# RMS norms of a two-layer backbone step: squares as each residual k tile is done, channel sum in column form, k outside in the product that follows

## The chip, the cores and the metric

The kernel runs on one core of one Trainium2 chip. The metric is the device time of one execution in microseconds (us), shown as the median of the runs. The core's engines are called PE (TensorE), DVE (VectorE), ACT (ScalarE), POOL (GpSimd) and SP (SyncE, which only issues transfers here). Each runs its own instruction list in order, and they are held together by semaphores.

## What is computed

The reference is one inference step with two layers over 128 context and 512 latent tokens of width 1024. Layer 0 mixes tokens by a gated DeltaNet and channels by a dense SwiGLU; layer 1 mixes by a short gated convolution and channels by a top-2-of-8 expert SwiGLU.

```
def rmsnorm(x, w):
    y = x * lax.rsqrt(jnp.mean(x * x, axis=-1, keepdims=True) + NORM_EPS)
    return y * w
for i in range(DEPTH):
    sh1, sc1, g1, sh2, sc2, g2 = ...
    h = rmsnorm(x, p["norm_w"][i, 0]) * (1 + sc1) + sh1
    x = x + g1 * mixer(h)
    h = rmsnorm(x, p["norm_w"][i, 1]) * (1 + sc2) + sh2
    x = x + g2 * swiglu_or_experts(h)
return rmsnorm(x, p["final_norm"])
```

So there are five norms, called norm 0 to norm 4 here: 0 before the DeltaNet's input product, 1 before the dense SwiGLU, 2 before the convolution's input product, 3 before the router, 4 at the end.

## The kernel before

The residual `xT` lies in SBUF with channels on the partitions: eight k tiles (KT = 8) of 128 channels by T = 640 tokens. Products are made in *units*. A unit multiplies 256 output channels (m = 0, 1, two tiles of 128; at the end of an expert only one) with all k tiles, in two halves of 320 tokens. For accuracy each weight and each activation is split in a high and a low part, and three of the four cross products are made, so that a unit with eight k tiles has 2 x 8 x 3 x 2 = 96 matmuls (`unit`, L517 to L532). `square_units` and `expert` run the units in pairs; units alternate between two weight buffers and two halves of PSUM.

POOL splits the weights of each unit (`split`: high part L421, low part L424, which reads two SBUF tiles); it may begin with the next unit for a buffer when PE has done the unit before in it. SP loads the raw weights. DVE drains the units that add to the residual: `residual` (L1209) for the DeltaNet's output product and the convolution's output product, called through `out_units`, and a loop in `expert` (L1241) for the down projections, which come in five units (`DOWN`) of 2, 2, 2, 1 and 1 tiles with eleven k tiles each. In the expert layer the residual is added in `add_scattered` (L1590), tile by tile.

A norm is spread over three engines by three functions called `norm`:

- ACT squares the k tiles of `xT` into a pair of buffers `sq` (L888), after a single wait that the whole residual is done. After PE's sum it writes the root `ms`, 128x640 (L890).
- DVE adds the squares up in `rstd` (seven adds, L1142, all after the last residual instruction in its list), later takes the reciprocal of the 128x640 tile (L1145), and then makes for each k tile `hp` (x times weight times rstd, L1154) and, after ACT has made the rounded `a_hi` from it (L898), the rest `a_lo` (L1161). It counts `h_lo` per k tile.
- PE multiplies a 128x128 tile of ones with the sum in `rstd` (two matmuls of 320 columns, L584), which leaves the sum over all channels on every partition.

The first unit behind norms 0, 1 and 2 waits for `h_lo` k tile by k tile, but only in its m = 0 half:

```
for m in range(nm):
    for k in range(kts):
        if m == 0 and after is not None:
            pe.wait_ge(sem("h_lo"), KT * after + (k + 1))
```

Between the dense SwiGLU and norm 2 DVE also runs `modulation(1)` (L1186, L1192), which makes the scale tables `mod` and `alpha` of layer 1. In norm 0 the same function for layer 0 stands ahead of the adds.

## Time and profile before

| | |
|---|---|
| median of 3 runs | 3572.23 us (3570.23 to 3577.03) |
| span of the profiled execution | 3566.9 us |
| PE busy in it | 3105.9 us, 87% of the span |
| DVE, ACT, POOL busy | 39%, 24%, 31% |
| mean granted TensorE clock | 0.871 of full speed |

The profile is of one further execution, for which only the span from the first to the last instruction is known. That span is 5.3 us shorter than the median and 3.3 us shorter than the fastest run; what lies around it (start and end of the program) is not in the trace. The busy share of PE says that it is the engine with the most work, not that it never waits.

### The profile page before, as it was taken

The numbers are of one execution on the slowest core, as the hardware profiler recorded it, in microseconds if no ns is written. First come the engines' busy times: TensorE is split into PE (matmuls) and PEld (weight loads), VectorE is DVE, ScalarE is ACT, GpSimd is POOL, SyncE is SP. The second block draws the span as 40 slices with busy tenths as digits, with TensorE's granted clock in tenths as the row PEclk, the third lists the DMA queues.
The fourth block names the chain that finished last, engine by engine and source line by source line (L and its number), as shares of the span: only waits on it lengthen the run. The fifth ranks groups of instructions, "written<-read, shape, count | busy, mean of one in ns | idle before, by whom it ended". The sixth has DMA issues, their size and how long they took to land.

```text
span 3566.9 us, 51011 instructions
## 1 busy us (share of the span) xinstructions
PE 3105.9 (87%) x20306; PEld 2798.3 (78%) x20306; DVE 1386.0 (39%) x1990; ACT 871.5 (24%) x1266; POOL 1120.6 (31%) x365
## 2 busy tenths in 40 slices
PE   7699888888888887799998797678999999999995
PEld 3499777777777776699998787667878888888784
DVE  0400346654665462411111342453443443443344
ACT  0200223222223221210110200223333333433431
POOL 1256022202220241365665363023232332323320
PEclk9799678767876777899999898689999999999996
DMA  9233201110111020122222121034444444544541
GB/s 296 75 126 110 72 25 51 39 53 18 50 38 53 18 70 16 46 85 61 71 81 66 47 71 36 0 95 149 137 129 136 149 124 130 162 123 135 155 136 53
DMA packets 428010, 311.10 MB, mean 87 GB/s; under 512 B 12146, under 2 KB 393067, under 8 KB 427883
## 3 DMA queue, kind: packets, MB, share of 16 engines
q1 hardware_dynamic: 414698, 286.08, 27.0%
q10 hardware_dynamic: 13184, 23.07, 1.9%
q8 instruction: 110, 1.80, 0.2%
q14 instruction: 18, 0.14, 0.0%
HBM read 294.96 MB, written 14.16 MB: 87 GB/s over the span
## 4 chain that ended last, share of the span: by engine, by line
PE 36%; issue 32%; POOL 12%; DVE 4%; ACT 2%; DMA 1%; DVEq 0%; POOLq 0%; SPq 0%; ACTq 0%
PE psum L529 14%; POOL m_lo L380 9%; PE psum L513 7%; PE psum L666 2%; PE psum L683 2%; PE psum L658 2%; POOL w_hi L421 2%; PE psum L577 2%; PE psum L673 2%; PE psum L508 1%; PE psum L689 1%; POOL w_lo L424 1%; DVE xt L1357 1%; PE psum L776 1%; ACT vn L976 1%
## 5 line engine op out<-in xcount | busy, mean ns | idle before, releaser
L380 POOL TENSOR_TENSOR m_lo<-m_raw,m_hi 128x2048 fp32r<-128x2048 f32 (+1 forms) x81 | 356.5, 4401 | 787.0 <-ACT m_hi L1097 787.0
L760 PE MATMUL psum<-he_hi,m_hi 128*128 128x192 f32 x1584 | 452.7, 286 | 35.0 <-POOL m_lo L380 34.8
L760 PE MATMUL psum<-he_lo,m_hi 128*128 128x192 f32 x1584 | 449.5, 284 | 33.7 <-issue 33.7
L421 POOL TENSOR_TENSOR w_hi<-raw,zero 128x2048 fp32r<-128x2048 f32 (+2 forms) x68 | 249.2, 3665 | 681.5 <-PE psum L529 582.1
L529 PE MATMUL psum<-a_hi,w_hi 128*128 128x320 f32 x1728 | 400.6, 313 | 63.9 <-DVE a_lo L1161 32.8
L760 PE MATMUL psum<-he_hi,m_lo 128*128 128x192 f32 x1584 | 450.0, 284 | 0.0
L529 PE MATMUL psum<-a_lo,w_hi 128*128 128x320 f32 x1728 | 396.9, 311 | 0.0
L529 PE MATMUL psum<-a_hi,w_lo 128*128 128x320 f32 x1728 | 396.5, 311 | 0.0
L1097 ACT ACTIVATE m_hi<-m_raw 128x2048 fp32r<-128x2048 f32 (+1 forms) x164 | 290.4, 1771 | 351.0 <-DMA m_raw<-in_moe_w_dram 278.5
L457 POOL TENSOR_TENSOR ml<-lt,level 128x640 f32<-128x640 f32 x80 | 124.8, 1567 | 782.3 <-PE psum L513 782.1
L760 PEld LDWEIGHTS psum<-he_hi,m_hi 128*128 128x128 f32 x1584 | 320.0, 202 | 41.6 <-issue 41.0
L529 PEld LDWEIGHTS psum<-a_hi,w_hi 128*128 128x128 f32 x1728 | 290.9, 190 | 72.8 <-issue 41.1
L760 PEld LDWEIGHTS psum<-he_hi,m_lo 128*128 128x128 f32 x1584 | 320.0, 202 | 34.2 <-issue 34.2
L424 POOL TENSOR_TENSOR w_lo<-raw,w_hi 128x2048 fp32r<-128x2048 f32 (+2 forms) x68 | 329.3, 4843 | 5.3
L760 PEld LDWEIGHTS psum<-he_lo,m_hi 128*128 128x128 f32 x1584 | 319.6, 202 | 0.1
L529 PEld LDWEIGHTS psum<-a_lo,w_hi 128*128 128x128 f32 x1728 | 292.1, 190 | 0.0
L529 PEld LDWEIGHTS psum<-a_hi,w_lo 128*128 128x128 f32 x1728 | 291.9, 190 | 0.0
L380 DVE TENSOR_TENSOR m_lo<-m_raw,m_hi 128x2048 fp32r<-128x2048 f32 (+1 forms) x82 | 179.5, 2189 | 222.9 <-ACT m_hi L1097 222.9
L1608 DVE TENSOR_TENSOR hid_lo<-m_prod,hid_hi 128x192 fp32r<-128x192 f32 x99 | 147.2, 1486 | 42.6 <-ACT hid_hi L1116 42.6
L1605 DVE TENSOR_TENSOR m_prod<-m_sg,psum 128x192 f32<-128x192 f32 x99 | 35.0, 353 | 308.3 <-ACT m_sg L1114 307.0
L577 PE MATMUL psum<-cond,raw 128*128 128x2 f32 x768 | 120.5, 290 | 27.5 <-DMA raw<-in_mod_w_dram 15.7
L577 PEld LDWEIGHTS psum<-cond,raw 128*128 128x128 f32 x768 | 119.5, 247 | 29.7 <-issue 26.4
(289 smaller groups left out, 5240.2 us busy)
## 6 DMA issues: line engine op xcount, KB each, us to landing
m_raw<-in_moe_w_dram SPq DMA_DIRECT2D x274, 512.0 KB, 4.6
raw<-in_mod_w_dram SPq DMA_DIRECT2D x48, 512.0 KB, 3.9
raw<-in_ffn_w_dram SPq DMA_DIRECT2D x44, 512.0 KB, 4.9
mod_raw<-in_mod_w_dram SPq DMA_DIRECT2D x16, 1024.0 KB, 7.2
raw<-in_dn_w_in_dram SPq DMA_DIRECT2D x32, 512.0 KB, 4.4
m_raw<-in_moe_w_dram SPq DMA_DIRECT2D x54, 256.0 KB, 2.7
raw<-in_sc_w_in_dram SPq DMA_DIRECT2D x24, 512.0 KB, 4.4
projected<-stage ACTq DMA_DIRECT2D x16, 640.0 KB, 3.1
```

Source lines behind the costliest of these rows:

```text
L380: eng.tensor_tensor(m_lo[q][:, 0:n], m_raw[j % 2][:, 0:n], m_hi[q][:, 0:n].bitcast(F32), ALU.subtract)\
L421: pool.tensor_tensor(w_hi[s][:, 0:cols], raw[s][:, 0:cols], zero[:, :].broadcast_to([P, cols]), ALU.add)\
L424: pool.tensor_tensor(w_lo[s][:, 0:cols], raw[s][:, 0:cols], w_hi[s][:, 0:cols].bitcast(F32), ALU.subtract).then_inc(sem("split"), 1)
L457: pool.tensor_tensor(ml[:, d, :, :], lt[:, d, :, :], level[:, l, :].unsqueeze(1).broadcast_to([P, TT, P]), ALU.mult)\
L513: mm = pe.matmul(wide(k)[:, t * P:(t + 1) * P], lhs(t), rhs(t), start=True, stop=True)
L529: mm = pe.matmul(psum[:, 4 * s + 2 * m + a, 0:HALF], w[:, k, m, :], v[:, k, a * HALF:(a + 1) * HALF], start=(k == 0 and n == 0), stop=(k = ...
L577: mm = pe.matmul(psum[:, 7, bass.ds(h * (2 * MOD_PER_HEAD) + (MOD_COL + 2 * i), 2)], w[:, k, :], cond[:, k, :], start=(k == 0), stop=(k == ...
L658: pe.matmul(psum[R, 4 * d, 0:P], cv[:, 1, cols], st[:, kind, d, :], start=True, stop=True).then_inc(sem(f"ks{d}"), 1)
L666: pe.matmul(psum[:, 4 * d + 2, 0:CH], st[:, kind, d, :], qe[:, d, cols], start=True, stop=False)
L760: mm = pe.matmul(psum[:, q, g * CAP:(g + 1) * CAP], w[:, c:c + P], v[:, k, :], start=(k == 0 and n == 0), stop=(k == KT - 1 and n == 2))
L1097: act.activation(m_hi[q][:, 0:n], m_raw[j % 2][:, 0:n], ACT.Copy).then_inc(sem("m_high"), 1)
L1608: dve.tensor_tensor(hid_lo[:, j, :], m_prod[:, :], hid_hi[:, j, :].bitcast(F32), ALU.subtract)\
```

## The change

- **Squares early.** ACT's `norm` now waits before each square until that k tile's residual is done (`pair_done`, `down_done`, or `added` in norm 4). DVE's adds are taken out of its `norm` into `add_square`, which is called right behind the residual instructions of each unit (norms 1, 2, 3) or of each tile (norm 4, one tile behind). For norm 0 the adds stay where they were. The loops of DVE around them (`out_units`, and the loop over the two halves of the dense SwiGLU) are written out. In norm 2 the squares lie in `gate_pair` and the sum in `late_total`, since the usual places are still in use; elsewhere the sum is in `sq_total`.
- **Column form.** PE takes the sum of squares as the stationary side against one column of ones, in five matmuls of one column, so that the channel sums of the 640 tokens stand as 128x5. ACT takes the root of 128x5, DVE the reciprocal of 128x5. To get them back along the free axis, DVE multiplies the identity with that column for each of the five token tiles (128x640, into `hp`), PE multiplies ones with it (two matmuls of 320), and DVE copies the 128x640 result from PSUM into `rstd`.
- **k outside.** In units that wait for `h_lo`, the loop over k is outside and the one over m inside.

The diff, cut:

```
-                for m in range(nm):
-                    for k in range(kts):
+                tiles_ = [(m, k) for m in range(nm) for k in range(kts)] if after is None else \
+                    [(m, k) for k in range(kts) for m in range(nm)]
+                for m, k in tiles_:
                         if m == 0 and after is not None:
                             pe.wait_ge(sem("h_lo"), KT * after + (k + 1))
...
             def norm(q):   # tensor
                 pe.wait_ge(sem("sq_added"), (KT - 1) * (q + 1))
+                for t in range(TT):
+                    mm = pe.matmul(psum[:, 0, t:t + 1], square_sum(q)[:, t * P:(t + 1) * P], ones[:, 0:1],
+                                   start=True, stop=True)
+                mm.then_inc(sem("norm_sum"), 1)
+                pe.wait_ge(sem("rstd"), 3 * q + 2)
                 for a in range(2):
-                    mm = pe.matmul(psum[:, a, 0:HALF], ones[:, :], rstd[:, a * HALF:(a + 1) * HALF],
+                    mm = pe.matmul(psum[:, 2 + a, 0:HALF], ones[:, :], hp[:, 0, a * HALF:(a + 1) * HALF],
...
-            def norm(q, ready, count):   # scalar
-                act.wait_ge(sem(ready), count)
+            def norm(q, ready):
                 for k in range(KT):
+                    ready(k)
...
-                act.activation(two(ms[:, :]), halves(0), ACT.Sqrt, scale=1.0 / D, bias=eps[:, :])\
+                act.activation(rcol[:, :], psum[:, 0, 0:TT], ACT.Sqrt, scale=1.0 / D, bias=eps[:, :])\
...
+            def add_square(q, k):   # vector
+                if k == 0:
+                    return
+                dve.wait_ge(sem("squared"), KT * q + k + 1)
+                if k > 1:
+                    dve.wait_ge(sem("sq_added"), (KT - 1) * q + k - 1)
+                dve.tensor_tensor(square_sum(q), squares(q)[:, 0, :] if k == 1 else square_sum(q),
+                                  squares(q)[:, k % 2, :], ALU.add).then_inc(sem("sq_added"), 1)
...
-                dve.reciprocal(rstd[:, :], ms[:, :]).then_inc(sem("rstd"), 1)
+                dve.reciprocal(rcol[:, :], rcol[:, :]).then_inc(sem("rstd"), 1)
+                dve.wait_ge(sem("rstd"), 3 * q + 1)
+                dve.tensor_tensor(tiles(hp[:, 0, :]), ident.unsqueeze(1).broadcast_to([P, TT, P]),
+                                  rcol[:, :].unsqueeze(2).broadcast_to([P, TT, P]), ALU.mult).then_inc(sem("rstd"), 1)
+                dve.wait_ge(sem("norm_sum"), 2 * q + 2)
+                dve.tensor_copy(two(rstd[:, :]), halves(2)).then_inc(sem("rstd"), 1)
...
-            def out_units(u0, gmod):
-                with dve.Fori(0, 2) as i:
-                    for s in range(2):
-                        residual(i * 2 + (u0 + s), s, i * 4 + 2 * s, 2, gmod)
+            def out_units(u0, gmod, q):
+                for n in range(4):
+                    residual(u0 + n, n % 2, 2 * n, 2, gmod)
+                    for k in (2 * n, 2 * n + 1):
+                        add_square(q, k)
...
                     ins.then_inc(sem("added"), 1)
+                    if last and m > 0:
+                        add_square(4, m - 1)
```

The instruction lists show where things went. First DVE around the last unit of the DeltaNet's output product and norm 1 (`xT` is the residual, `sq` the squares, `same` holds the identity). Before:

```order
L1209 SCALAR_TENSOR_TENSOR xT<-psum,mod,xT 128x128
L1209 ISA
L1209 SCALAR_TENSOR_TENSOR xT<-psum,mod,xT 128x192
L1209 ISA
L1209 SCALAR_TENSOR_TENSOR xT<-psum,mod,xT 128x320
L1215 REGISTER_ALU
L1215 COMPARE_AND_BRANCH
L1142 TENSOR_TENSOR rstd<-sq 128x640
L1142 TENSOR_TENSOR rstd<-rstd,sq 128x640 x6
L1145 RECIPROCAL rstd<-ms 128x640
```

After:

```order
L1171 TENSOR_TENSOR sq_total<-sq_total,sq 128x640 x2
L1244 SCALAR_TENSOR_TENSOR xT<-psum,mod,xT 128x128
L1244 SCALAR_TENSOR_TENSOR xT<-psum,mod,xT 128x192
L1244 SCALAR_TENSOR_TENSOR xT<-psum,mod,xT 128x320
L1244 SCALAR_TENSOR_TENSOR xT<-psum,mod,xT 128x128
L1244 SCALAR_TENSOR_TENSOR xT<-psum,mod,xT 128x192
L1244 SCALAR_TENSOR_TENSOR xT<-psum,mod,xT 128x320
L1171 TENSOR_TENSOR sq_total<-sq_total,sq 128x640 x2
L1176 RECIPROCAL rcol<-rcol 128x5
L1178 TENSOR_TENSOR hp<-same,rcol 128x640
L1181 COPY rstd<-psum 128x640
```

Six of the seven adds moved ahead, between the residual instructions of the units; two are behind the last unit. The reciprocal of 640 elements became three instructions.

DVE behind the last down projection, in norm 2, with the change:

```order
L1171 TENSOR_TENSOR late_total<-late_total,gate_pair 128x640
L1222 TENSOR_TENSOR mod<-psum,col 128x96
L1228 SCALAR_TENSOR_TENSOR alpha<-mod,col 128x16 x2
L1176 RECIPROCAL rcol<-rcol 128x5
L1178 TENSOR_TENSOR hp<-same,rcol 128x640
L1181 COPY rstd<-psum 128x640
```

The last add now stands ahead of `modulation(1)`, whose three instructions stand ahead of the reciprocal.

PE at norm 0 and the first product behind it, before:

```order
L584 MATMUL psum<-rstd,ones 128x320 [waits sq_added,mod_evac]
L584 MATMUL psum<-rstd,ones 128x320
L529 MATMUL psum<-a_hi,w_hi 128x320 [waits h_lo,split,rms]
L529 MATMUL psum<-a_hi,w_hi 128x320
L529 MATMUL psum<-a_lo,w_hi 128x320 x2
L529 MATMUL psum<-a_hi,w_lo 128x320 x2
L529 MATMUL psum<-a_hi,w_hi 128x320 [waits h_lo]
```

and after:

```order
L597 MATMUL psum<-ones,sq_total 128x1 [waits sq_added,mod_evac]
L597 MATMUL psum<-ones,sq_total 128x1 x4
L602 MATMUL psum<-hp,ones 128x320 [waits rstd]
L602 MATMUL psum<-hp,ones 128x320
L542 MATMUL psum<-a_hi,w_hi 128x320 [waits h_lo,split,rstd]
L542 MATMUL psum<-a_hi,w_hi 128x320
L542 MATMUL psum<-a_lo,w_hi 128x320 x2
L542 MATMUL psum<-a_hi,w_lo 128x320 x2
L542 MATMUL psum<-a_hi,w_hi 128x320 x2
L542 MATMUL psum<-a_lo,w_hi 128x320 x2
L542 MATMUL psum<-a_hi,w_lo 128x320 x2
L542 MATMUL psum<-a_hi,w_hi 128x320 [waits h_lo]
```

Five one-column matmuls and a wait were added, and per wait for `h_lo` PE now has twelve matmuls to do instead of six.

## Rows read from the trace of the kernel before

**Rows 1.** What PE waited for: line, waited for, total us, times, longest.
```profile
PE psum L584 <- DVE rstd L1142: 73.3, 5, 22.0
```

**Rows 2.** Timeline of DVE at norm 1: start, us, engine, line, instructions, idle before.
```profile
1444.25 2.18 DVE L1209 SCALAR_TENSOR_TENSOR xT<-psum,mod,xT 128x128 f32 x6 [11.90 <-PE psum L529]
1447.85 5.13 DVE L1142 TENSOR_TENSOR rstd<-sq 128x640 f32<-128x640 f32 x1 [1.43 <-ACT sq L888]
1453.78 5.47 DVE L1142 TENSOR_TENSOR rstd<-rstd,sq 128x640 f32<-128x640 f32 x6 [0.80 <-ACT sq L888]
1462.68 4.15 DVE L1145 RECIPROCAL rstd<-ms 128x640 f32<-128x640 f32 x1 [3.42 <-ACT ms L890]
1466.86 1.94 DVE L1154 SCALAR_TENSOR_TENSOR hp<-xT,alpha,rstd 128x128 f32<-128x128 f32 x4
```

**Rows 3.** Timeline of ACT at norm 1.
```profile
1446.46 1.36 ACT L888 ACTIVATE sq<-xT 128x640 f32<-128x640 f32 x2 [67.58 <-DVE xT L1209]
```

**Rows 4.** Timeline of PE at norm 1.
```profile
1459.31 2.50 PE L584 MATMUL psum<-rstd,ones 128*128 128x320 f32 x4 [15.33 <-DVE rstd L1142]
1469.88 0.87 PE L529 MATMUL psum<-a_hi,w_hi 128*128 128x320 f32 x2 [8.06 <-DVE a_lo L1161]
1470.55 0.73 PE L529 MATMUL psum<-a_lo,w_hi 128*128 128x320 f32 x2
1471.08 0.73 PE L529 MATMUL psum<-a_hi,w_lo 128*128 128x320 f32 x2
...
1481.63 0.56 PE L529 MATMUL psum<-a_hi,w_hi 128*128 128x320 f32 x2 [0.83 <-DVE a_lo L1161]
```

**Rows 5.** Timeline of POOL, last two splits ahead of norm 1.
```profile
1429.98 3.60 POOL L421 TENSOR_TENSOR w_hi<-raw,zero 128x2048 fp32r<-128x2048 f32 x1 [5.75 <-PE psum L529]
...
1444.13 3.60 POOL L421 TENSOR_TENSOR w_hi<-raw,zero 128x2048 fp32r<-128x2048 f32 x1 [5.82 <-PE psum L529]
1447.81 4.49 POOL L424 TENSOR_TENSOR w_lo<-raw,w_hi 128x2048 fp32r<-128x2048 f32 x1
```

**Rows 6.** Timeline of POOL: the next split, when norm 1's first unit is done.
```profile
1490.84 3.60 POOL L421 TENSOR_TENSOR w_hi<-raw,zero 128x2048 fp32r<-128x2048 f32 x1 [38.54 <-PE psum L529]
```

**Rows 7.** Stretches behind norms 0 and 1: busy by engine (x), PEclk, DMA, GB/s.
```profile
147.00:151.00 4.00, 3.98 (x13) 3.24 (x13) 3.93 (x9) 2.25 (x4) 0.00 (x0) 0.50 0.00 0
...
1469.90:1476.00 6.10, 6.08 (x19) 4.94 (x20) 5.99 (x14) 3.38 (x6) 0.00 (x0) 0.51 0.00 0
```

**Rows 8.** Timeline of DVE at norm 2.
```profile
1957.89 1.13 DVE L1241 SCALAR_TENSOR_TENSOR xT<-psum,mod,xT 128x128 f32<-128x128 f32 x3 [8.54 <-PE psum L529]
...
1959.42 2.23 DVE L1192 SCALAR_TENSOR_TENSOR alpha<-mod,col 128x16 f32<-128x16 f32 x2
...
1980.73 1.94 DVE L1154 SCALAR_TENSOR_TENSOR hp<-xT,alpha,rstd 128x128 f32<-128x128 f32 x4
```

**Rows 9.** Timeline of POOL at norm 2.
```profile
1957.93 3.60 POOL L421 TENSOR_TENSOR w_hi<-raw,zero 128x2048 fp32r<-128x2048 f32 x1 [1.35 <-PE psum L529]
1961.61 4.50 POOL L424 TENSOR_TENSOR w_lo<-raw,w_hi 128x2048 fp32r<-128x2048 f32 x1
```

**Rows 10.** Timeline of DVE at norm 3.
```profile
2250.87 2.18 DVE L1209 SCALAR_TENSOR_TENSOR xT<-psum,mod,xT 128x128 f32 x6 [11.90 <-PE psum L529]
...
2256.10 5.47 DVE L1142 TENSOR_TENSOR rstd<-rstd,sq 128x640 f32<-128x640 f32 x6 [0.80 <-ACT sq L888]
```

**Rows 11.** Timeline of DVE at norm 4.
```profile
3524.91 1.01 DVE L1590 SCALAR_TENSOR_TENSOR xT<-psum,mod,xT 128x128 f32<-128x128 f32 x2 [1.93 <-PE psum L735]
...
3529.00 5.47 DVE L1142 TENSOR_TENSOR rstd<-rstd,sq 128x640 f32<-128x640 f32 x6 [0.80 <-ACT sq L888]
```

**Rows 12.** Line L812, small matmuls at the low clock: ns min/median/max, first, last start.
```profile
L812 PE MATMUL psum<-tab,tri x4: 414/415/436, 408.4 to 409.0; 128*128 128x40 f32 x4
```

**Rows 13.** Timeline of ACT and DVE in the router: small instructions.
```profile
2311.38 0.24 ACT L1081 ACTIVATE sm<-sm 128x40 f32<-128x40 f32 x1 [26.35 <-DVE sm L1495]
...
2311.87 0.19 DVE L1498 RECIPROCAL sm<-sm 128x5 f32<-128x5 f32 x1
```

More of the change, by code:

```diff
@@ L103, in build @@
         rtb = sb("rtb", [P, E])
+        rcol = sb("rcol", [P, TT])
         wrt_hi = sb("wrt_hi", [P, KT, E], F32R)
@@ L120, in build @@
             yT = sb("yT", [P, KT, T], F32, fin)
+        with ExitStack() as late:
+            sb("late_gap", [P, (2 * KT - 1) * T], F32, late)
+            late_total = sb("late_total", [P, T], F32, late)
         with ExitStack() as dense:
@@ L227, in two, with squares, square_sum @@
             return ap.rearrange("p (a c) -> p a c", a=2)
+        def squares(q):
+            return gate_pair if q == 2 else sq
+        def square_sum(q):
+            return late_total[:, :] if q == 2 else sq_total[:, :]
         SPANS = [(0, TC, 0), (TC, T, 1)]
@@ L881, in _, with pair_done, down_done @@
         def _(act):
-            def norm(q, ready, count):
-                act.wait_ge(sem(ready), count)
+            def norm(q, ready):
                 for k in range(KT):
+                    ready(k)
                     if k >= 2:
                         act.wait_ge(sem("sq_added"), (KT - 1) * q + max(1, k - 2))
-                    act.activation(sq[:, k % 2, :], xT[:, k, :], ACT.Square).then_inc(sem("squared"), 1)
-                act.wait_ge(sem("norm_sum"), q + 1)
-                act.activation(two(ms[:, :]), halves(0), ACT.Sqrt, scale=1.0 / D, bias=eps[:, :])\
+                    act.activation(squares(q)[:, k % 2, :], xT[:, k, :], ACT.Square).then_inc(sem("squared"), 1)
+                act.wait_ge(sem("norm_sum"), 2 * q + 1)
+                act.activation(rcol[:, :], psum[:, 0, 0:TT], ACT.Sqrt, scale=1.0 / D, bias=eps[:, :])\
                     .then_inc(sem("rms"), 1)
+            def pair_done(u0):
+                return lambda k: act.wait_ge(sem("evacuated"), u0 + k // 2 + 1)
+            def down_done(u0):
+                return lambda k: act.wait_ge(sem("evacuated"), u0 + [n for n, m0, nm in DOWN if m0 <= k < m0 + nm][0] + 1)
             def norm_hi(q, n):
@@ L1023, in _ @@
                     mod_rows(i, s, False)
-            norm(0, "x_evac", TT)
+            norm(0, lambda k: act.wait_ge(sem("x_evac"), TT))
             act.wait_ge(sem("alpha"), 2)
@@ L1060, in _ @@
             act.activation(act_hi[:, 0:H, :], oall[:, :, :], ACT.Copy).then_inc(sem("o_hi"), 1)
-            norm(1, "evacuated", U_FFN)
+            norm(1, pair_done(U_DN_OUT))
             norm_hi(1, 1)
@@ L1064, in _ @@
                 expert(e * PER_EXPERT + U_FFN)
-            norm(2, "evacuated", U_SC_IN)
+            act.wait_ge(sem("multiplied"), U_FFN + PER_EXPERT + FT)
+            norm(2, down_done(U_FFN + PER_EXPERT + FT))
             act.wait_ge(sem("alpha"), 4)
@@ L1076, in _ @@
             act.activation(a_hi[:, :, :], cy[:, :, :], ACT.Copy).then_inc(sem("cy_hi"), 1)
-            norm(3, "evacuated", U_MOE)
+            norm(3, pair_done(U_SC_OUT))
             norm_hi(3, 1)
@@ L1131, in _ @@
                 routed(x)
[L1132 removed]
+            norm(4, lambda k: act.wait_ge(sem("added"), n_items * KT + (k + 3)))
         @block.vector
         def _(dve):
[L1137 to L1146 removed]
+            def add_square(q, k):
[6 more added lines that the diff above has]
+                                  squares(q)[:, k % 2, :], ALU.add).then_inc(sem("sq_added"), 1)
+            def norm(q, w_of, out=None):
+                dve.wait_ge(sem("rms"), q + 1)
+                dve.reciprocal(rcol[:, :], rcol[:, :]).then_inc(sem("rstd"), 1)
[4 more added lines that the diff above has]
+                dve.tensor_copy(two(rstd[:, :]), halves(2)).then_inc(sem("rstd"), 1)
+                dve.wait_ge(sem("rstd"), 3 * q + 3)
                 n = q % 2
@@ L1227, in gate_unit, with expert @@
                                   ALU.subtract).then_inc(sem("act_lo"), 1)
-            def expert(u0, n0):
+            def expert(u0, n0, last):
                 with dve.Fori(0, 5) as i:
@@ L1244, in expert @@
                     ins.then_inc(sem("evacuated"), 1)
+                    for k in range(m0, m0 + nm) if last else ():
+                        add_square(2, k)
             def conv(dst, src, w, tag, n0):
@@ L1398, in _ @@
             modulation(0)
+            for k in range(KT):
+                add_square(0, k)
             norm(0, a_of(0))
@@ L1449, in _ @@
                 .then_inc(sem("act_lo"), 1)
-            out_units(U_DN_OUT, 16)
+            out_units(U_DN_OUT, 16, 1)
             norm(1, a_of(1))
-            with dve.Fori(0, N_FFN) as e:
-                expert(e * PER_EXPERT + U_FFN, e * FT)
+            for e in range(N_FFN):
+                expert(e * PER_EXPERT + U_FFN, e * FT, e == N_FFN - 1)
             modulation(1)
@@ L1583, in gathered_low, with add_scattered @@
                                       ALU.subtract).then_inc(sem("he_lo"), 1)
-            def add_scattered(x):
+            def add_scattered(x, last=False):
                 for m in range(KT):
@@ L1629, in _ @@
                 routed(x)
-            add_scattered(n_items)
-            dve.memset(small[:, 0, 0:1], 0.0).then_inc(sem("moe_done"), 1)
+            add_scattered(n_items, True)
+            add_square(4, KT - 1)
             norm(4, lambda k, w: col1[:, C_FINAL + k:C_FINAL + k + 1], out=yT)
```

27 lines of the change are left out of this document (9 added, 18 removed).

## The prediction

> **What bounds the kernel now.** I read the waits of PE first, then the timeline of each engine around each norm. PE has most of the work, so what can be won without taking work from it is time in which it stands still. The waits name it: the ones-matmul of the norms waited 73.3 us in five places for DVE's adds [rows 1], and PE's first unit behind a norm stands still again, 8.06 us ahead of it and a little ahead of each tile [rows 4]. The timelines show that nothing else runs beside these waits: at norm 1 the last unit ends at about 1444.1, when POOL and DVE are released [rows 2, 5], and PE's next product starts at 1469.88 [rows 4]. So at each norm the end is set by this chain: last residual, squares, adds, sum, root, reciprocal, `hp`, `a_hi`, `a_lo`, first unit. A microsecond taken from it is a microsecond of the kernel, as all later work is released by other work, and in the stage behind it PE has the longest turn: units follow each other every 14.15 us while POOL's two splits need 8.2 [rows 5].
>
> **Squares early.** Call the end of the last add T, measured against the end of the last residual instruction.
>
> Norm 1. Before: residual ends 1446.43, T = 1453.78 + 5.47 = 1459.25 [rows 2]. With the change only adds 6 and 7 are left there. The first add took 5.13 us where the same instruction later takes 0.9 [rows 2]; it began at 1447.85, right behind the start of POOL's second split at 1447.81, and ended 0.7 after that one's end at 1452.30 [rows 5]. So an add with both inputs in SBUF waits for a running POOL instruction to end, then takes 0.7. Square 6 is there at 1447.2 [rows 3], in the first split; add 6 runs from 1447.73 to 1448.4. If the second split slips by that, it ends at 1452.9 and T is 1453.6; if not, 1453.0. The Trainium skill (SBUF — State Buffer, "SBUF: two separate sides") says that of a DVE instruction with two SBUF inputs and a GpSimd one that reads SBUF, whichever starts first holds a shared port pair for its whole length and the other blocks; by that the split does slip. I take 1453.6: **5.6 us** saved (6.2 if it does not slip).
>
> Norm 3. The same list, but POOL has no unit left to split. Residual ends 2253.05, T was 2261.57 [rows 10]. Now: two squares, 1.4, and one add behind them, 0.9, so T = 2255.4: **6.1 us**.
>
> Norm 2. Residual ends 1959.02; DVE then ran `modulation(1)` to 1961.65, and `hp` began at 1980.73 [rows 8]. Now add 7 (its square ready at 1959.8) waits for POOL's first split to end at 1961.53 [rows 9] and ends at 1962.2. The three modulation instructions come behind it, beside PE's five matmuls and ACT's root; but `alpha` has two SBUF inputs too (2.23 us for two 128x16 tiles, until a POOL instruction ended [rows 8, 9]), so it waits for the second split, 1962.3 to 1966.8. The reciprocal comes at about 1967.2, and from there the chain below needs 4.6: `hp` at 1971.8, **9.0 us** earlier.
>
> Norm 4. Residual ends 3525.92, T was 3534.47 [rows 11]. Now add 6 (0.8, its square long done) and add 7 end at 3527.6: **6.9 us**.
>
> Norm 0. The adds stay behind `modulation(0)`, in the same order: 0.
>
> **Cover of the moved adds.** Six adds and squares now lie inside the units. DVE's residual part of a unit takes 2.2 us of a turn of 14.15 [rows 2, 5]; two adds that each sit out a POOL instruction add at most 3.6 + 4.5 + 1.4 = 9.5. That is 11.7, still hidden. If the cover were gone, each microsecond above 14.15 would stop PE in every such unit. ACT is idle there (67.58 us before the first square [rows 3]). In norm 4 a tile comes every 2.9 us, 1.93 idle and 1.01 residual [rows 11]; an add of 0.9 fits.
>
> **Column form.** Before, T to `hp` took 1466.86 - 1459.25 = 7.6 us [rows 2], of which 2.5 PE [rows 4] and 4.15 the reciprocal. Now: five fp32 matmuls of one column. No row shows one; the nearest are L812's, 128x128 weights and 40 columns at the low clock: four records for two instructions, started 0.2 apart, the last 0.41 long [rows 12]. Ten records give 9 x 0.2 + 0.4, with their start 2.3. Root 0.24, reciprocal 0.19 [rows 13] (a 128x40 and the same size). Identity times column 0.9, as an add [rows 2]; PE 0.1 + 2.5 [rows 4]; the copy, 640 elements, again 0.9; handovers 0.1. Sum 7.3: **0.3 us** saved per norm at norms 0, 1, 3, 4 (in norm 2 it is in the 9.0). The chain swaps one long DVE instruction for a second trip through PE and gains nearly nothing. Bounds: if the records run twice as fast, 1 us less; if they cost twice as much, 2.1 us more.
>
> The Trainium skill (FP8 and Floating Point Precision, "TensorE Precision Notes") says that true fp32 takes four passes through the array. The trace has two records for an fp32 instruction, four for two matmuls [rows 4]. Four times the five matmuls would be twenty records, the upper bound just given, and the sum over five norms would be 10 us worse. I go by the rows.
>
> **k outside** (norms 0, 1, 2; norm 3 is followed by the router, which waits for everything, norm 4 by transposes). In norm 1 the first unit ran from 1469.88 to about 1490.8 [rows 4, 6], 20.9 us. Its seventh k tile began at 1481.63 [rows 4], so DVE and ACT deliver `a_lo` every 11.75 / 6 = 1.96 us; behind the last tile come 48 more matmuls, m = 1, at the high clock. PE needs for its twelve matmuls 3.2 us at 1.2 GHz (two start 0.53 apart [rows 4]) or 1.76 at 2.4 GHz (a unit of 96 in 14.15 [rows 5], 0.147 each). So at the low clock PE becomes the slower one, at the high clock it keeps up. The granted clock was 0.51 in the first 6.1 us of that unit, and 0.50 in the first 4 of the one behind norm 0 [rows 7]; the latter I take for norm 2 too. Norm 1: 6.0 us cold hold 22.5 matmuls, the other 73.5 take 10.8, together 16.8: **4.1 us** saved. Norms 0 and 2: 4 us hold 15, the other 81 take 11.9, together 15.9: **5.0 us** each. The floor is `a_lo` of the last tile and twelve matmuls, 1.0 + 1.8 behind that seventh tile (the last needs no `hp` of a next one, half a step), 14.5 in all, so at most 6.4 each. The units behind are released by PE and by POOL, which starts its next split when this unit ends and has 6 us to spare, so all of it moves forward.
>
> **Sum.** 0: 5.3. 1: 5.6 + 0.3 + 4.1 = 10.0. 2: 9.0 + 5.0 = 14.0. 3: 6.4. 4: 7.2. Together **42.9 us**. The span would go from 3566.9 to 3524.0; the median lies 5.3 above the span, and I keep that distance: 3572.2 - 42.9 = **3529.3 us**. What one measurement can tell from no change is about 0.2%, 7 us.
>
> **Rivals.**
>
> A. *The column matmuls cost double.* Twenty passes instead of ten, 2.1 us in each of five norms: 3529.3 + 10.5 = 3540. For: no row has a moving side of one column. Against: L812's records. 8%.
>
> B. *k outside brings nothing,* because PE at the low clock with twelve matmuls per tile stays behind, or the clock rises later than before: 14.1 us lost, 3543. Against: PE was busy for nearly all of those first microseconds already (6.08 of 6.10 [rows 7]), so there is little to rise sooner or later for. 5%.
>
> C. *The change does not bring the squares forward:* ACT's per-tile waits or the buffer waits hold them until the last unit. Then 27.6 + 0.3 of the gain is gone and about 15 stay: 3557. Against: the waits name earlier counts, and ACT is idle. 3%.
>
> D. *Slower than before: the adds inside the units hold DVE longer than PE's turn.* Each add sits out POOL's instructions, the next residual comes late, and PE waits for its PSUM. DVE's turn would be 2.2 + two adds; it decides above 14.15, that is from 6 us per add on. To eat the gain of 43 in the thirteen units with adds (4, 5 and 4 in norms 1, 2, 3) it needs 3.3 us beyond, 7.6 per add; at 8.5 per add it is 5.0 us each, 65 in all, 3529 + 65 = 3594. For: an add took 5.13 against one POOL instruction [rows 2]. Against: that instruction was the longer of the two, and the turns behind a down unit are longer still. 3%.
>
> **How the numbers follow.** My forecast has 81%. Its own bounds: T of norm 1 0.6 better, k outside 1 better, the column 1 better in five places and other handovers, 8 in all: 3521; the other way 1 us in each of ten places: 3539. The range takes in A and B and some spread of the runs (3570 to 3577 before): **3519 to 3545**. It leaves out C, D and a rest. Faster by over 0.2%: 0.94, which is the forecast with A, B, C and less a rest for what I have not seen; within 0.2%: 0.03; slower: 0.03.
>
> **What would show it.** In the profile of the changed kernel: T some 7.2 us behind the last residual at norm 1, 2.4 at norm 3, 1.7 at norm 4; one add of about 5 us beside POOL's second split at norms 1 and 2; T to `hp` at 7.3; five matmuls in 2.3; the first unit behind norms 0, 1 and 2 at 16 to 17 us instead of 20.9; PE's units in the product ahead of norm 1 still 14.15 apart. Wrong would be: T to `hp` above 8.5, adds that end after the next unit, a first unit above 18, or a stage away from the norms that grows.

## The result, and the profile after

The changed kernel takes **3476.5 us** (median of 4 runs, 3472.3 to 3479.2) against 3572.9 of the kernel before in the same job (4 runs, 3570.2 to 3577.0): a ratio of 0.973, 95% interval 0.971 to 0.975. The profiled execution has a span of 3475.1 us instead of 3566.9, 91.8 less. (The two differences are not the same because the profiled execution of the kernel before was a short one; see the heads below.) I had predicted 3529.3 and a range of 3519 to 3545: the sign was right, but the gain is 96 us instead of 43, and the time lies below the range.

Both programs do the same work in the same order, so a start in one trace can be set against the same start in the other. The table cuts the span into six at such marks (ends of named PE work), in us:

| stretch | before | after | difference | predicted |
|---|---|---|---|---|
| to the end of norm 0's first unit | 167.6 | 163.0 | -4.6 | -5.3 |
| to the end of the second DeltaNet head | 490.4 | 502.6 | **+12.2** | 0 |
| heads 3 to 8 | 709.1 | 709.2 | 0.1 | 0 |
| norms 1, 2, 3, with what lies between, to the first expert tile | 1001.1 | 968.6 | -32.5 | -30.4 |
| loop over the routed experts, first to last L760 tile | 1090.7 | 1031.0 | **-59.7** | 0 |
| behind it: last down projection, norm 4, output | 107.9 | 100.7 | -7.2 | -7.2 |

The stretches with norms give 44.3 us where 42.9 were predicted. Two stretches in which the change alters nothing moved too: that is the miss. (The heads are the eight heads of the DeltaNet.)

First what was predicted. What PE waited for, in the changed kernel (line, waited for, total us, times, longest), answers to [rows 1]:

```profile
PE psum L597 <- DVE sq_total L1171: 39.1, 4, 22.0
...
PE psum L602 <- DVE hp L1178: 9.0, 5, 3.2
...
PE psum L597 <- DVE late_total L1171: 4.5, 1, 4.5
```

The waits for the adds fell from 73.3 to 39.1 + 4.5; 22.0 of it is norm 0, where nothing was moved. DVE at norm 1 (start, us, instructions, idle before), against [rows 2]:

```profile
1440.49 6.53 DVE L1171 TENSOR_TENSOR sq_total<-sq_total,sq 128x640 f32<-128x640 f32 x2 [0.81 <-ACT sq L906]
1451.58 2.17 DVE L1244 SCALAR_TENSOR_TENSOR xT<-psum,mod,xT 128x128 f32<-128x128 f32 x6 [4.57 <-PE psum L542]
1454.56 6.45 DVE L1171 TENSOR_TENSOR sq_total<-sq_total,sq 128x640 f32<-128x640 f32 x2 [0.80 <-ACT sq L906]
1463.69 0.19 DVE L1176 RECIPROCAL rcol<-rcol 128x5 f32<-128x5 f32 x1 [2.68 <-ACT rcol L908]
1463.91 0.82 DVE L1178 TENSOR_TENSOR hp<-same,rcol 128x640 f32<-128x640 f32 x1
1467.33 0.82 DVE L1181 COPY rstd<-psum 128x640 f32<-128x640 f32 x1 [2.59 <-PE psum L602]
1468.19 1.94 DVE L1190 SCALAR_TENSOR_TENSOR hp<-xT,alpha,rstd 128x128 f32<-128x128 f32 x4
```

The residual ends at 1453.75 and the last add at 1461.01: T is 7.26 behind it (predicted 7.2), and `hp` begins 7.18 after T (predicted 7.3). (Of the seven adds five lie inside the units, and two behind the last; that six moved, as the text ahead of the prediction and the prediction have it, is a miscount. It enters no term.) The adds inside the units end long before the next residual: 1440.49 + 6.53 = 1447.02 against 1451.58, still 14.08 behind the one before. POOL at the same norm, against [rows 5, 6]:

```profile
1451.69 3.60 POOL L433 TENSOR_TENSOR w_hi<-raw,zero 128x2048 fp32r<-128x2048 f32 x1 [5.36 <-PE psum L542]
1455.37 4.96 POOL L436 TENSOR_TENSOR w_lo<-raw,w_hi 128x2048 fp32r<-128x2048 f32 x1
1488.01 3.60 POOL L433 TENSOR_TENSOR w_hi<-raw,zero 128x2048 fp32r<-128x2048 f32 x1 [27.68 <-PE psum L542]
```

The two adds end 0.68 behind POOL's second split (1455.37 + 4.96 = 1460.33): one of them sat it out. PE behind norm 1, against [rows 4]:

```profile
1461.06 2.29 PE L597 MATMUL psum<-ones,sq_total 128*128 128x1 f32 x10 [9.52 <-DVE sq_total L1171]
1464.79 2.50 PE L602 MATMUL psum<-hp,ones 128*128 128x320 f32 x4 [1.44 <-DVE hp L1178]
1471.20 0.87 PE L542 MATMUL psum<-a_hi,w_hi 128*128 128x320 f32 x2 [3.91 <-DVE a_lo L1197]
```

Ten records in 2.29 us (predicted 2.3). The first unit runs from 1471.20 to about 1488.0, 16.8 us instead of 20.9. DVE at norms 2 and 4, against [rows 8, 11]:

```profile
1957.10 2.32 DVE L1171 TENSOR_TENSOR late_total<-late_total,gate_pair 128x640 f32<-128x640 f32 x1 [0.80 <-ACT gate_pair L906]
...
1959.62 4.28 DVE L1228 SCALAR_TENSOR_TENSOR alpha<-mod,col 128x16 f32<-128x16 f32 x2
1963.93 0.19 DVE L1176 RECIPROCAL rcol<-rcol 128x5 f32<-128x5 f32 x1
...
1968.43 1.94 DVE L1190 SCALAR_TENSOR_TENSOR hp<-xT,alpha,rstd 128x128 f32<-128x128 f32 x4
```

```profile
3440.33 1.01 DVE L1630 SCALAR_TENSOR_TENSOR xT<-psum,mod,xT 128x128 f32<-128x128 f32 x2 [1.20 <-PE psum L753]
3441.25 1.75 DVE L1171 TENSOR_TENSOR sq_total<-sq_total,sq 128x640 f32<-128x640 f32 x2
```

`alpha` sits out a POOL split again (4.28 us), as foreseen. The add at norm 2 took 2.32: it waited for the first split alone, and is not the add of about 5 us that my list of signs had there.

Now what was not. Part 3 of the page (queue, kind: packets, MB, share) for the kernel before, then for the changed one:

```profile
q8 instruction: 110, 1.80, 0.2%
```

```profile
q8 instruction: 38, 0.62, 0.1%
```

q8 brings PE's code: its packets have 16,384 bytes each, and in straight code the trace has 254 to 256 PE instructions between two of them (in the kernel before at 1648.8, 1667.3, 1686.0 and 1704.5). Before, 69 of the 110 packets fall between 2492 and 3485, in the loop over the experts, nine in a round. Between 2452 and 3430 the changed kernel has one q8 packet. PE's waits in that loop, before:

```profile
PE psum L760 <- issue: 33.7, 8, 4.5
PE psum L760 <- POOL m_lo L380: 27.8, 18, 2.8
PE psum L719 <- POOL m_lo L380: 6.2, 4, 1.7
```

and after:

```profile
PE psum L737 <- POOL m_lo L392: 14.8, 9, 2.5
PE psum L778 <- POOL m_lo L392: 9.4, 9, 1.2
PE psum L778 <- DVE m_lo L392: 1.3, 4, 0.4
```

Eight waits for "issue", one at each jump back of nine rounds, are gone, 33.7 us; the other waits fell by 8.5. One of the eight in PE's timeline, before (eighth matmul of the round):

```profile
2610.70 0.27 PE L760 MATMUL psum<-he_hi,m_hi 128*128 128x192 f32 x1
2615.34 0.25 PE L760 MATMUL psum<-he_lo,m_hi 128*128 128x192 f32 x1 [4.37 <-issue]
2615.43 0.28 PE L760 MATMUL psum<-he_hi,m_lo 128*128 128x192 f32 x1
```

And the loop as a stretch (us, busy by engine, PEclk, DMA share, GB/s), before and after:

```profile
2368.29:3458.98 1090.69, 1022.78 (x7248) 911.46 (x7247) 461.16 (x513) 396.91 (x452) 342.79 (x78) 0.97 0.47 137
```

```profile
2343.37:3374.36 1030.99, 1005.39 (x7249) 894.92 (x7247) 477.11 (x513) 396.29 (x453) 343.56 (x78) 0.99 0.50 143
```

PE is busy 17.4 us less at the same number of matmuls: the granted clock is 0.97 against 0.99. So 33.7 + 8.5 + 17.4 = 59.6 of the 59.7. This is a sum of what differs; which of its terms hang on one cause is for the experiments.

### The profile page after: what moved, and what is told of

It reads as the page before. It is cut to its first block, busy times and chain, and to the rows that moved or that the text cites. A ratio compares the mean times of both kernels' runs of the same rounds, so it can differ in the third digit from the quotient of the medians.

```text
span 3475.1 us, 51066 instructions
## 1 busy us (share of the span) xinstructions
PE 3105.1 (89%) x20356; PEld 2801.9 (81%) x20356; DVE 1412.7 (41%) x1999; ACT 868.6 (25%) x1266; POOL 1125.0 (32%) x365
## 4 chain that ended last, share of the span: by engine, by line
PE 36%; issue 31%; POOL 12%; DVE 4%; ACT 2%; DMA 1%; DVEq 0%; POOLq 0%; SPq 0%; ACTq 0%
PE psum L542 15%; POOL m_lo L392 9%; PE psum L525 7%; PE psum L684 2%; PE psum L701 2%; PE psum L676 2%; POOL w_hi L433 2%; PE psum L691 2%; PE psum L590 2%; PE psum L707 1%; POOL w_lo L436 1%; DVE xt L1395 1%; PE psum L794 1%; ACT vn L1002 1%; PE psum L520 1%
## 5 line engine op out<-in xcount | busy, mean ns | idle before, releaser
L778 PE MATMUL psum<-he_hi,m_hi 128*128 128x192 f32 x1584 | 444.1, 280 | 17.9 <-POOL m_lo L392 16.4
L778 PE MATMUL psum<-he_lo,m_hi 128*128 128x192 f32 x1584 | 441.4, 279 | 0.0
L778 PE MATMUL psum<-he_hi,m_lo 128*128 128x192 f32 x1584 | 441.1, 278 | 0.0
L778 PEld LDWEIGHTS psum<-he_hi,m_hi 128*128 128x128 f32 x1584 | 311.0, 196 | 23.7 <-issue 22.4
L778 PEld LDWEIGHTS psum<-he_hi,m_lo 128*128 128x128 f32 x1584 | 311.6, 197 | 0.0
L778 PEld LDWEIGHTS psum<-he_lo,m_hi 128*128 128x128 f32 x1584 | 311.2, 196 | 0.4
L1650 DVE TENSOR_TENSOR hid_lo<-m_prod,hid_hi 128x192 fp32r<-128x192 f32 x99 | 165.1, 1667 | 42.6 <-ACT hid_hi L1143 42.6
L525 PE MATMUL psum<-xx,ml 128*128 128x128 f32 x800 | 104.0, 279 | 39.3 <-DVE xt L1395 24.2
```

Of the source, the lines that this page charges most:

```text
L525: mm = pe.matmul(wide(k)[:, t * P:(t + 1) * P], lhs(t), rhs(t), start=True, stop=True)
L778: mm = pe.matmul(psum[:, q, g * CAP:(g + 1) * CAP], w[:, c:c + P], v[:, k, :], start=(k == 0 and n == 0), stop=(k == KT - 1 and n == 2))
L1650: dve.tensor_tensor(hid_lo[:, j, :], m_prod[:, :], hid_hi[:, j, :].bitcast(F32), ALU.subtract)\
```

## The experiments

**Theory: code placement.** The change puts five matmuls (20 instructions with their weight loads, as an fp32 matmul has two records of each) ahead of each of norms 0 to 3 in PE's list. By that the loop over the experts (1706 PE records a round in the trace; the 1726 of the expectations is my count in the compiled program, which no trace shows) starts 80 instructions later within its 256-instruction blocks. Before, its blocks did not stay loaded from round to round; after, they do. **Rival:** the edits of the norms made the loop faster (their order, their buffers, the time at which it starts). For the heads: the edits cost 12 us there, or it is chance.

### Padding, and nothing else

The edit of e1, at the router:

```
+            for _ in range(20):
+                pe.matmul(psum[:, 3, 0:1], ones[:, :], ones[:, 0:1], start=True, stop=True)
             pe.wait_ge(sem("sel"), 1)
```

e1, the kernel before with 80 instructions more. Expected:

> The kernel before with nothing changed but 20 matmuls of one column (80 instructions in PE's list, as many as the change adds ahead of the expert loop) while PE waits for the router. Theory 'code placement': the routed expert loop's 1700 PE instructions then lie in the code buffer as in the changed kernel, so q8 goes from 110 packets to about 38, no 4.5 us stop of PE at each jump back, and the time falls by 55 to 62 us: 3511 to 3518. Rival 'the norm edits themselves (their order, their buffers, the point in time at which the loop starts) made the loop faster': q8 stays at 110 packets, 3573 within 3.

Measured: 3517.2 us, ratio 0.986 (0.984 to 0.988). q8 38, no wait for issue at L760, 1028.5 us in the loop, 62 less. Not one line of the norms was touched. The rival falls: code placement alone makes this loop faster.

e2, the changed kernel with the same lines and `range(44)`, 176 instructions more, so that it stands as before plus one whole block. Expected:

> The changed kernel with 44 matmuls of one column (176 instructions) in the same place, so that the expert loop starts 256 instructions, one 16,384-byte packet of code, later than in the kernel before. Theory 'code placement': the refetches are back, q8 about 111 packets, and the time is that of the changed kernel plus 55 to 62: 3532 to 3539. That would leave for the five norms and the DeltaNet heads together -34 to -41 against before. Rival 'norm edits': 3477 within 3.

Measured: 3535.6 us, 0.991 (0.990 to 0.993). q8 111, issue 32.1 us in 8, loop 1084.4. The gain of the loop is gone, 53.4 of the 59.7 us. The padding is not free here: it costs 13.7 us ahead of the loop, read as the difference of the two traces between norm 3 and the first expert tile.

### Single parts

e3, k outside alone:

```
-                for m in range(nm):
-                    for k in range(kts):
+                tiles_ = [(m, k) for m in range(nm) for k in range(kts)] if after is None else \
+                    [(m, k) for k in range(kts) for m in range(nm)]
```

> The kernel before with the one edit k outside; PE's list keeps its length. My prediction's terms: norm 0 -5.0, norm 1 -4.1, norm 2 -5.0 in the trace, q8 at 110 packets, 3559. Rival B, k outside brings nothing: 3573. If the 12 us by which the DeltaNet heads' first pass grew in the changed kernel hang on what PE does in norm 0's first unit, they show here too: 3571.

Measured: 3555.9 us, 0.996 (0.995 to 0.998), q8 110, loop 1085.4. In the trace -3.8 at norm 0 and -8.6 at norms 1 and 2: 12.4 for my 14.1.

e4, squares early alone (the changed kernel with these lines back in the old form, and m outside):

```
-                for t in range(TT):
-                    mm = pe.matmul(psum[:, 0, t:t + 1], square_sum(q)[:, t * P:(t + 1) * P], ones[:, 0:1],
-                                   start=True, stop=True)
...
+                    mm = pe.matmul(psum[:, a, 0:HALF], ones[:, :], square_sum(q)[:, a * HALF:(a + 1) * HALF],
...
+                dve.reciprocal(rstd[:, :], rstd[:, :]).then_inc(sem("rstd"), 1)
```

> Squares early alone, with the sum, root and reciprocal in the old form (128x640, no column) and m outside; PE's list keeps its length. My prediction's terms: norm 0 0, norm 1 -5.6, norm 2 -9.0 less what modulation(1) then hides, norm 3 -6.1, norm 4 -6.9: about -27, 3545, q8 at 110 packets, and the heads unchanged. Rival C, squares not early: 3573. Rival 'the heads' growth is a chance event of the clock': the heads differ here too, in either direction.

Measured: 3547.4 us, 0.993 (0.992 to 0.995). q8 110, loop 1092.1, norms 1 to 3 -22.1 and norm 4 -6.9 in the trace, 29.0 for my 27.6. The second head ended 10.2 us late here, though nothing of norm 0 is changed.

e5, squares early and k outside, without the column form (the same edit as e4, with k outside kept):

> The changed kernel without the column form: squares early and k outside stay, sum, root and reciprocal are 128x640 again. PE's list is as long as in the kernel before, so by 'code placement' q8 is at 110 packets and the expert loop runs as before: 3571 less 27 less 12 = 3532, and within 3 of the run with 176 instructions of padding, since the column form in itself is worth 0.3 us per norm. Rival 'norm edits': the loop stays fast, q8 38, 3478.

Measured: 3530.9 us, 0.988 (0.986 to 0.991). q8 110, loop 1087.8. Norms 1 to 3 give -32.4, the changed kernel -32.5: the column form is worth nothing there, and the other edits of the norms leave the loop as slow as it was. This run is the gain of the edits without the loop's: 44.0 us by the medians of its job (3574.9 to 3530.9).

e13, the column form alone:

```
+                for t in range(TT):
+                    mm = pe.matmul(psum[:, 0, t:t + 1], rstd[:, t * P:(t + 1) * P], ones[:, 0:1],
+                                   start=True, stop=True)
...
-                dve.reciprocal(rstd[:, :], ms[:, :]).then_inc(sem("rstd"), 1)
+                dve.reciprocal(rcol[:, :], rcol[:, :]).then_inc(sem("rstd"), 1)
```

> The kernel before with the column form alone. By its own chain it is worth 1.5 us in five norms (my prediction's term). Theory 'code placement': its five matmuls in each of four norms are the 80 instructions, so it brings the whole loop gain too: q8 38, -55 to -62, 3511 to 3518. Rival 'norm edits other than the column form did it': 3571, q8 110.

Measured: 3523.0 us, 0.984 (0.982 to 0.987). q8 38, loop 1039.7. The edit whose own chain is worth 1.5 us by my sum brings 55 (3578.3 to 3523.0 in its job), 51 of it in the loop. That is the low end of the 55 to 62 that I expected; the time lies above my 3511 to 3518, as the kernel before was slower in this job.

### Where the loop starts

The same padding with other counts: e8 `range(10)` and e9 `range(30)` at the router; e12 `range(15)`, e14 `range(36)`, e15 `range(30)` and e16 `range(54)` at the start of PE's list, where it waits for the first transfer:

```
+            pe.wait_ge(sem("ones"), 1)
+            for _ in range(15):
+                pe.matmul(psum[:, 3, 0:1], ones[:, :], ones[:, 0:1], start=True, stop=True)
             pe.wait_ge(sem("params"), 16 * 16)
             pe.wait_ge(sem("masks"), 1)
-            pe.wait_ge(sem("ones"), 1)
```

> The kernel before with 10 matmuls (40 instructions) of padding at the router. Theory: nine blocks of 256 instructions (eight that the 1726-instruction loop touches, and the one fetched ahead) do not stay, eight do; the loop touches seven only if it starts in the first 66 of a block's 256 instructions. As 0 misses and 80 hits, of 40 and 120 at most one can hit. Hit: q8 38, about -55; miss: q8 110, 3570. Rival 'any more than a few instructions help, or the hit comes from the router's timing': both 40 and 120 give 38 packets and -55.

> The same with 30 matmuls (120 instructions). Theory: hit (q8 38, about -55) only if the run with 40 missed; miss: q8 110 or 111, 3570. Rival: 38 packets and -55, as with 80.

> The kernel before with 15 matmuls of one column (60 instructions) at the very start of PE's list, in the 16 us in which PE waits for its first transfer, so nothing near the router changes. Theory 'code placement': 40 and 80 hit, so 60 does: q8 38, -50 to -62, 3513 to 3524. Rival 'the padding worked through the router's timing': q8 110, 3573.

> The kernel before with 36 matmuls of one column (144 instructions) at the start of PE's list. Theory: a miss again (q8 110, PE's jump back 3.3 to 4.0 us instead of 0.21), but the first instruction of the loop now has some 130 of its block behind it instead of the few that it had in the kernel before, so PE has work until the next block is there: no stop of 4 us at L760, and the loop takes about what it took with 120, 1061 us (1055 to 1068) instead of 1084 to 1092: 3545 to 3555 in all. Rival 'a miss costs the same wherever it falls': 1084 to 1092 in the loop, 3573 in all.

> The kernel before with 30 matmuls of one column (120 instructions) at the start of PE's list instead of at the router. Theory 'only the stop costs': q8 about 110, jump back 3.3 to 4.0 us, no stop, loop 1028 to 1048, so 3515 to 3530 in all. Rival 'the position 120 in itself costs half of it': 1061 in the loop again, 3545 to 3553.

> The kernel before with 54 matmuls (216 instructions) there, which takes PE some 7 us beyond its wait for the first transfer. 54 to 80 instructions of the loop's first block are left. Theory 'the stop comes when PE has used up the first block's rest before the next block is there': these are 27 to 40 matmuls, 3 to 4.5 us at the high clock, against a stop of 4.4 with 14 to 40 left; so the stop shrinks to 1 to 3 us and the loop takes 1050 to 1075. Rival 'any refetch with the same stop': 1084 to 1092. Rival 'no stop outside the last few instructions': 1028 to 1048.

Measured, with the others; "jump" is the time of PE's branch at the end of a round, from the trace's records of it, "stop" the waits for issue at the loop's first product; "busy" PE's busy time in the loop, and the rest of the loop is time in which PE stands idle. A "hit" in the expectations is a start at which the code stays loaded:

| kernel | added | q8 | jump, us | stop, us in all | loop, us | busy, us | ratio to before |
|---|---|---|---|---|---|---|---|
| before | 0 | 110 | 3.3 to 4.0 | 33.7 | 1090.7 | 1022.8 | |
| e5 | 0 | 110 | 3.3 to 3.8 | 34.6 | 1087.8 | 1024.1 | 0.988 (0.986 to 0.991) |
| e8 | 40 | 38 | 0.21 | 0 | 1047.8 | 1021.3 | 0.989 (0.986 to 0.991) |
| e12 | 60 | 38 | 0.21 | 0 | 1046.6 | 1019.7 | 0.985 (0.983 to 0.988) |
| e1 | 80 | 38 | 0.21 | 0 | 1028.5 | 1004.7 | 0.986 (0.984 to 0.988) |
| changed | 80 | 38 | 0.21 | 0 | 1031.0 | 1005.4 | 0.973 (0.971 to 0.975) |
| e9 | 120 | 110 | 3.3 to 3.8 | 0 | 1061.5 | 1033.7 | 0.994 (0.992 to 0.996) |
| e15 | 120 | 119 | 3.3 to 3.9 | 0 | 1060.1 | 1028.8 | 0.994 (0.992 to 0.996) |
| e14 | 144 | 119 | 3.4 to 3.9 | 0 | 1033.4 | 1008.5 | 0.985 (0.982 to 0.989) |
| e16 | 216 | 120 | 3.4 to 3.9 | 17.4 | 1063.8 | 1022.1 | 0.998 (0.996 to 0.999) |
| e2 | 256 | 111 | 3.3 to 3.8 | 32.1 | 1084.4 | 1021.3 | 0.991 (0.990 to 0.993) |

e8 and e9: of 40 and 120 just one hit, as it must be by the theory, by which seven blocks and the one fetched ahead stay and nine do not. (That a block is fetched ahead is argued; a round that refetches has nine packets.) In time both missed my expectations: e8 gained 39 us in place of 55, and e9, expected at 3570, came out at 3553.2 against 3574.9. e12, at 3524.4 by the edge of its 3513 to 3524: as to whether the code stays, the place of the padding does not matter.

e14 refuted half of my theory. It refetches in every round, and its jumps back take 3.4 to 3.9 us, but the loop is as fast as with resident code (1033.4): PE has matmuls queued that cover the jump. What costs waiting time is the *second* stop: in the kernel before, in e2 and in e5, it comes in each of the eight rounds behind exactly 7 matmuls of the new round. My reading is that there the jump's target block ends, and the next one is not there yet. e16 tests this: its blocks end 40 instructions, 20 matmuls, later. Its stops come behind exactly 27 matmuls, and are shorter, as expected (line, waited for, total, times, longest):

```profile
PE psum L760 <- issue: 17.4, 8, 2.6
```

17.4 us in place of 33.7, 2.0 less each; twenty matmuls at 0.11 us are 2.2. With 144 and 120 the block ends 56 and 68 matmuls later, 6 us and more, and no stop is left. e15 answers the other question: 120 costs 27 us more than 144 in both places where I put it, without a stop. So my theory that only the stop costs is refuted, and its rival came true.

The column "busy" shows what the theory covers. PE's idle time in the loop, loop less busy, follows the stops: 63.1 to 67.9 us with the full stops (before, e5, e2), 41.7 in e16, and 23.8 to 31.4 without. PE's busy time, for the same matmuls, does not follow the code. Three stretches of the loop, of e8 (code resident), of e9 and of e14 (both refetch, no stop):

```profile
2380.02:3427.78 1047.76, 1021.30 (x7249) 910.02 (x7247) 476.97 (x513) 395.29 (x452) 343.16 (x78) 0.97 0.49 141
```

```profile
2378.58:3440.07 1061.49, 1033.70 (x7248) 920.47 (x7247) 477.33 (x513) 396.04 (x452) 343.30 (x78) 0.96 0.49 141
```

```profile
2374.18:3407.57 1033.39, 1008.49 (x7248) 896.72 (x7248) 477.87 (x513) 397.07 (x453) 343.36 (x78) 0.98 0.50 144
```

e8 lost its stops and kept the kernel before's busy time and granted clock (0.97); of the 28.1 us by which e9 is slower than e14, 25.2 are busy time. So of the 59.7 us the experiments show the cause of the 42.2 of waits (33.7 + 8.5). The 17.4 of busy time go with a higher granted clock, and what sets that in this loop stays open: with resident code it was 1004.7 (e1), 1005.4 (changed), 1013.1 (e13), 1019.7 (e12) and 1021.3 (e8).

### The heads

> The kernel before once more, with a profile of its own. Theory 'the first passes of the DeltaNet heads vary from execution to execution with the granted clock': the stretch from the heads' start to norm 1 is 0 to 12 us longer than in the profile shown first, and all else, the expert loop above all, is within 6 us of it, with q8 at 110. Rival 'the edits made the heads longer': the stretch is as before within 0.5.

e11 is the kernel before, unedited, in a second profile: span 3571.8, loop 1086.5. From the last matmul of the DeltaNet's small input product to the end of the second head, in the first profile of the kernel before, in e11, and in the changed kernel:

```profile
402.90:658.00 255.10, 213.94 (x1324) 184.50 (x1324) 142.07 (x264) 76.91 (x152) 42.06 (x28) 0.73 0.15 46
```

```profile
404.70:669.80 265.10, 223.49 (x1324) 191.74 (x1324) 142.43 (x263) 77.16 (x152) 41.52 (x28) 0.69 0.15 44
```

```profile
399.90:665.60 265.70, 223.52 (x1323) 191.73 (x1324) 142.46 (x264) 77.13 (x152) 41.47 (x28) 0.69 0.15 44
```

The unedited kernel has the same 10 us, at the same granted clock of 0.69 instead of 0.73. In the fifteen profiles other than the first it takes 257.2 to 265.7 us. So the change need not have made the heads longer; the profile that I read before predicting was the shortest of all there. Set against e11, the changed kernel's span is 96.7 us shorter, close to the 96.4 of the medians: 46.8 in the stretches with norms, 55.5 in the loop, and 5.6 lost in the heads, all of that in heads 3 to 8 but 0.4. So a stretch of the table at the start is good to some 5 us only, and in the heads to 10.

### A version meant to beat both

e10 is the changed kernel with norm 0's squares, adds, sum and `rstd` ahead of `modulation(0)`: DVE is idle there until 114 us, and its adds behind it took 18 us of PE's wait of 22.0.

```
-            modulation(0)
             for k in range(KT):
                 add_square(0, k)
+            rstd_of(0)
+            modulation(0)
             norm(0, a_of(0))
...
+                    if s == 3:
+                        norm_sum(0)
+                norm_back(0)
```

> A version meant to beat both: the changed kernel with all of norm 0 up to rstd done ahead of modulation(0), whose 114 us DVE and ACT idle through. PE's list keeps its length, so q8 stays at 38. In the changed kernel DVE is at hp of norm 0 at 143.4 and PE's first unit ends near 162. Now hp can begin at 118.1 but shares its time with POOL's four splits, which end at 131.8; the first unit should end at 144 to 146, less 4.8 us that the nine small matmuls put into PE's modulation: -10 to -13, 3464 to 3467. Rival: DVE and POOL block each other further, -5; or the modulation hides nothing and PE's detour costs more, 0.

Measured: **3456.9 us**, 0.968 (0.965 to 0.972) of before. Its first unit ends at 152.0 instead of 163.0, 11 us earlier, with q8 38 and 1032.5 in the loop. I had expected 10 to 13 less than the changed kernel, 3464 to 3467; the span is 19.8 less, 11 of it here and 4.9 in heads 3 to 8, where nothing was changed. Its ratio (0.965 to 0.972) and the changed kernel's (0.971 to 0.975) come from different jobs and just touch, so by the times alone that it beats the changed kernel is likely and not certain; the 11 us of norm 0 are the part that the trace shows. DVE there:

```profile
120.63 13.74 DVE L1210 SCALAR_TENSOR_TENSOR hp<-xT,alpha,rstd 128x128 f32<-128x128 f32 x4
134.29 1.00 DVE L1217 SCALAR_TENSOR_TENSOR a_lo<-hp,mod,a_hi 128x128 fp32r<-128x128 f32 x2
```

Four small instructions, elsewhere 1.94 us, take 13.74: three of them sit out one each of the splits that POOL runs from 120.56 to 133.56. That seems to be what still bounds it; no run tests it.

## Why the prediction was right and where it was wrong

**The waits and their chain: right.** T was 7.26 us behind the residual at norm 1 (7.2 predicted), 2.6 at norm 3 (2.4), 1.66 at norm 4 (1.7). `hp` came 9.6 earlier at norm 2 (9.0). That a microsecond of this chain is one of the kernel held: the stretches with norms gave 44.3 for the 42.9 of the chains' sum.

**Column form: right in itself.** T to `hp` 7.18 to 7.25 (7.3), five matmuls 2.3. Rival A falls: ten records, not twenty. The Trainium skill's four passes (FP8 and Floating Point Precision, "TensorE Precision Notes") do not show as a price here; the row with ten records decides.

**k outside: right, slightly high.** 4.0, 4.2 and 5.0 us at norms 0, 1 and 2 in the changed kernel (5.0, 4.1, 5.0), 3.8 and 8.6 alone. Rival B falls.

**Cover of the moved adds: right.** Units stayed 14.08 apart, rivals C and D fall. POOL's second split did not start 0.7 later, as I had it. It started 0.08 behind the first, took 4.96 us instead of 4.49, and so ended 6.58 behind the residual instead of 5.87: by my branch "it slips", and so is T. The Trainium skill (SBUF — State Buffer, "SBUF: two separate sides") says that of a DVE instruction with two SBUF inputs and a GpSimd one that reads SBUF the one that starts first holds a shared port pair for its whole length, and the other waits. The trace agrees in that DVE's second add ended only behind the split; the 0.47 us that the split grew by fit a wait for the end of the add before it, but the row does not show where in the split they were lost.

**The step that failed is "Sum".** It carried the edits' 42.9 us from 3566.9 to a span of 3524.0 as if nothing else could change. The edits gave 44.3. The rest of the program gave 47.5 more: 59.7 in the expert loop, less 12.2 in the heads. Of the first, the 42.2 us of waits come from the term "column form", where I counted what five matmuls take in time, 2.3 us, and not what they are in PE's list: 20 instructions ahead of everything that follows, per norm. The instruction lists showed them, and the page showed 110 packets on q8 and a wait of 33.7 us for "issue" in eight places; I read neither. The other 17.4 went with the granted clock, and their cause is open. The second comes from taking one profile as the kernel: its heads were about 10 us shorter than in a second profile of the same kernel. My sign "a stage away from the norms that grows" did appear, and for this reason it was no sign of the change. The 5.3 us that I kept between span and median were of the same kind: each run's time lies only some 1.8 above its span (3476.86 and 3475.1 in the profiled run of the changed kernel), and the rest, about 3.5, was the short execution. By the medians the miss is 52.8 us: the 47.5, the 1.4 by which the edits gave more, and 3.9 since the changed kernel's median lies only 1.4 above its span.

**The range** took in bounds of the edits only. It had no case in which a stage away from the norms gains.

The Trainium skill says of this (Runtime: NRT & Kernel Launch, "Instruction fetch mechanics") that PE's instruction memory holds 2048 instructions and is refilled in blocks of 256, and that a taken branch to a target outside "the current 2-page window" makes the engine wait for a fetch. The runs agree with the size of a block (254 to 256 between packets), with eight blocks that stay (of 40 and 120 one hit), and with a wait at a jump to code that is not loaded (3.3 to 4.0 us against 0.21). They do not agree with a window of two pages: in the changed kernel PE jumps back over some 1700 instructions, more than six blocks, in 0.21 us and without a fetch. And the wait that cost time was the one behind the jump, as e14 and e16 show: after 7 matmuls of the round, where by my reading the target's own block was used up before the next had come.

## What to carry to other kernels

Whoever adds or removes instructions ahead of a long loop moves the loop against its code blocks: look at the instruction queue's packets per round and at waits for "issue" that recur once a round, before and after, and compare an edit with a padded version of the old kernel before crediting it. Here one edit worth nothing in itself brought 55 us. Without it, 40 instructions that do nothing brought 39, and 120 brought only 22. Sum an edit against one profile only after a second profile of the same kernel has shown what its stretches vary by.

## What the runs showed of the hardware

- A jump back takes PE 0.21 us when its target is loaded and 3.3 to 4.0 when not. Queued matmuls can cover all of that: the loop of e14 took 1033.4 us with it, and 1028.5 to 1047.8 without.
- Idle time of PE in the loop: 63 to 68 us with eight stops of about 4.2 us (33.7 in all before), 41.7 with eight of 2.2, and 24 to 31 with none, in kernels with the same work there.
- The loop's other part does not follow the code. PE was busy in it for 1021.3 to 1027.3 us with the full stops (six profiles), 1004.7 to 1021.3 with the code resident (six), and 1008.5 to 1033.7 with refetches but no stop (three), the less the higher the granted clock: 0.99 at 1004.7, 0.96 at 1033.7.
- With code resident, the loop's time still spread from 1028.5 to 1047.8 us, with 1225 to 1352 starts of a matmul 0.16 to 0.25 us behind the one before; in the original position six profiles gave 1084.4 to 1092.1. Some of this spread may belong to the position; that was not separated.
